# Expert weights of a mixture-of-experts stage: each 1 MB unit loaded by two 512 KB transfers with a semaphore each, waited for and freed by halves

## The reference, cut to what matters

```
def expert_choice_moe(h, w_router, w_gate, w_up, w_down):      # h: 1 x 512 x 1024
    cap = CAPACITY_FACTOR * S // N_EXPERTS                      # 64 rows for each of 16 experts
    aff = jax.nn.softmax((h @ w_router).astype(jnp.float32), axis=-1)
    gates, idx = lax.top_k(aff.swapaxes(1, 2), cap)
    xin = jax.vmap(lambda hb, ib: hb[ib])(h, idx)
    a = jnp.einsum("becd,edf->becf", xin, w_gate)               # each of the three weights is 1024 x 1024
    b = jnp.einsum("becd,edf->becf", xin, w_up)
    y = jnp.einsum("becf,efd->becd", jax.nn.silu(a) * b, w_down)
    y = y * gates.astype(y.dtype)[..., None]
    ... # rows are added back at idx; the last step of the program is an RMS norm of the result
```

## Time and profile before

| what | value |
|---|---|
| time, median of 3 runs | 2463.63 us (2462.45 to 2464.12) |
| the profiled execution's own time | 2466.73 us |
| its span, first to last instruction | 2464.9 us |
| TensorE busy | 2389.1 us, 97% of the span |
| DVE, ACT, POOL busy | 1211.2, 860.4 and 37.2 us |
| DMA | 387.64 MB, mean 157 GB/s over the span |
| transfers of units | 192 of 1024 KB |

### The profile page before, as it was taken

How to read it: one execution, slowest core, us unless ns; L and a number is a source line. 1 busy time by engine, 2 the same in 40 slices (tenths; PEclk the granted TensorE clock), 3 DMA queues, 4 the chain that set the end, 5 groups by cost and what they waited for, 6 DMA issues and landing times. The chain is left out here.

```text
span 2464.9 us, 34565 instructions
## 1 busy us (share of the span) xinstructions
PE 2389.1 (97%) x14242; PEld 1847.2 (75%) x14242; DVE 1211.2 (49%) x1867; ACT 860.4 (35%) x1325; POOL 37.2 (2%) x57
## 2 busy tenths in 40 slices
PE   6999999999999999999999999999998999999997
PEld 5994889999999988677788888876897753333323
DVE  3798556552455343674664565653543422233223
ACT  4125653321233233584542344356444311101101
POOL 0000000000000001100000000000000100000000
PEclk8999999999999999999999999999999999999999
DMA  5248432221112142002232232220341669999996
GB/s 232 86 125 306 172 119 86 68 83 47 60 61 80 65 164 83 31 2 69 94 101 96 94 104 93 82 62 1 107 145 41 256 279 408 421 421 421 421 421 286
DMA packets 74251, 387.64 MB, mean 157 GB/s; under 512 B 8576, under 2 KB 12928, under 8 KB 43264
## 3 DMA queue, kind: packets, MB, share of 16 engines
q1 hardware_dynamic: 74112, 385.66, 41.6%
HBM read 380.22 MB, written 2.10 MB: 155 GB/s over the span
## 5 line engine op out<-in xcount | busy, mean ns | idle before, releaser
L285 DVE TENSOR_TENSOR WLO<-RAW,WHI 128x1024 fp32r<-128x1024 f32 (+3 forms) x221 | 273.1, 1236 | 627.8 <-ACT WHI L272 627.7
L329 PE MATMUL PS<-XNH,WHI 128*128 128x384 f32 (+2 forms) x1816 | 572.7, 358 | 7.2 <-PEq L2839 2.6
L329 PE MATMUL PS<-XNH,WLO 128*128 128x384 f32 (+2 forms) x1816 | 564.8, 353 | 0.0
L329 PE MATMUL PS<-XNL,WHI 128*128 128x384 f32 (+2 forms) x1816 | 564.5, 353 | 0.0
L272 ACT ACTIVATE WHI<-RAW 128x1024 fp32r<-128x1024 f32 (+3 forms) x221 | 236.2, 1069 | 754.1 <-PE PS L329 715.1
L329 PEld LDWEIGHTS PS<-XNH,WHI 128*128 128x128 f32 x1816 | 335.3, 188 | 40.7 <-issue 10.0
L329 PEld LDWEIGHTS PS<-XNL,WHI 128*128 128x128 f32 x1816 | 335.2, 188 | 31.4 <-issue 3.4
L329 PEld LDWEIGHTS PS<-XNH,WLO 128*128 128x128 f32 x1816 | 335.1, 188 | 29.2
L3049 PE MATMUL PS<-RAWM,XS 128*64 128x512 f32 x1024 | 237.2, 599 | 9.0 <-DMA RAWM<-experts 8.4
L3049 PEld LDWEIGHTS PS<-RAWM,XS 128*64 128x64 f32 x1024 | 68.2, 136 | 139.2 <-issue 105.1
L329 PE MATMUL PS<-HH,WHI 128*128 128x384 f32 (+1 forms) x528 | 158.0, 353 | 0.1
(11 more groups left out here) (379 smaller groups left out, 2754.5 us busy)
## 6 DMA issues: line engine op xcount, KB each, us to landing
RAWM<-experts SPq DMA_DIRECT2D x191, 1024.0 KB, 15.0
RAW<-up SPq DMA_DIRECT2D x88, 512.0 KB, 3.3
ADAW<-ada SPq DMA_DIRECT2D x26, 1024.0 KB, 6.5
RAW<-down SPq DMA_DIRECT2D x32, 704.0 KB, 4.0
ADAG<-ada SPq DMA_DIRECT2D x14, 1024.0 KB, 11.3
RAW<-pw SPq DMA_DIRECT2D x24, 512.0 KB, 3.8
ADAL<-ada SPq DMA_DIRECT2D x8, 1024.0 KB, 6.3
RAW<-qkv SPq DMA_DIRECT2D x12, 512.0 KB, 3.5
```

The costliest lines, as they stand in the source:

```text
L285: dve.tensor_tensor(lo[:, 0:to.length], prog.RAW[:, at % RAWS, 0:to.length], f32(hi[:, 0:to.length]), ALU.subtract).then_inc(prog.weights_ ...
L329: last = pe.matmul(prog.PS[:, to, at:at + b - a], w, x[:, k, a:b], start=(k == 0 and n == 0), stop=(k == g.k - 1 and n == 2))
```

## The change

Each unit is loaded by two transfers. The first takes columns 0 to 1023 of all 128 partitions, the second columns 1024 to 2047, so that a partition's row in a transfer is 4 KB in place of 8 KB. Each half of a slot has a semaphore of its own (28 in place of 14). TensorE waits for a half ahead of the block that is in it, and adds one to `done` after each block; SP waits for half of the former unit ahead of each half's transfer. ACT's waits on `done` count twice as many. The arithmetic and its order are the same.

```diff
+def load_half(prog, sp, g, c):
+
+    moe = prog.moe
+    slot, src = moe.slots[g], prog.dram["experts"][g][:, c * UNIT // 2:(c + 1) * UNIT // 2]
+    to = moe.whole[slot]
+    if len(to.shape) == 3:
+        to, src = to[:, 4 * c:4 * c + 4, :], src.rearrange("p (a b) -> p a b", b=TOK - LAT)
+    else:
+        to = to[:, c * UNIT // 2:(c + 1) * UNIT // 2]
+    sp.dma_start(to, src).then_inc(prog.expert_landed[2 * slot + c], 16)
+
 def load_unit(prog, sp, g):
-    moe = prog.moe
-    slot, src = moe.slots[g], prog.dram["experts"][g]
-    if len(moe.whole[slot].shape) == 3:
-        src = src.rearrange("p (a b) -> p a b", b=TOK - LAT)
-    sp.dma_start(moe.whole[slot], src).then_inc(prog.expert_landed[slot], 16)
+    for c in range(2):
+        load_half(prog, sp, g, c)
...
             for g in range(N_SLOTS, UNITS):
-                sp.wait_ge(done, moe.before[g] + 1)
-                load_unit(prog, sp, g)
+                for c in range(2):
+                    sp.wait_ge(done, 2 * moe.before[g] + 1 + c)
+                    load_half(prog, sp, g, c)
...
             def unit(g, j, x, ps):
                 slot = moe.slots[g]
-                pe.wait_ge(prog.expert_landed[slot], 16 * moe.use[g])
                 for n in range(2):
+                    pe.wait_ge(prog.expert_landed[2 * slot + n], 16 * moe.use[g])
                     k = 2 * j + n
                     for half in range(2):
                         last = pe.matmul(ps[64 * half:64 * half + 64, :], x(k), moe.half[slot](2 * n + half),
                                          start=(k == 0), stop=(k == KD - 1))
-                last.then_inc(done, 1)
+                    last.then_inc(done, 1)
 
             def last_down(pair):
...
-                pe.wait_ge(prog.expert_landed[slot], 16 * moe.use[first_down(LAST_E) + pair])
                 for k in range(KD):
+                    if k % HALF_K == 0:
+                        pe.wait_ge(prog.expert_landed[2 * slot + k // HALF_K], 16 * moe.use[first_down(LAST_E) + pair])
...
-                last.then_inc(done, 1)
+                    if k % HALF_K == HALF_K - 1:
+                        last.then_inc(done, 1)
...
-                act.wait_ge(done, first_up(e) + PART)
+                act.wait_ge(done, 2 * (first_up(e) + PART))
```

More of the change, by code:

```diff
@@ L114, in __init__ @@
         self.gap_landed = nc_sem("ada_gap_landed")
-        self.expert_landed = [nc_sem(f"expert_landed{i}") for i in range(N_SLOTS)]
+        self.expert_landed = [nc_sem(f"expert_landed{i}") for i in range(2 * N_SLOTS)]
         first = self.expert_landed[-1].num + 1
@@ L3216, in _ @@
                 keep_rows(0, k)
-            act.wait_ge(done, PART)
+            act.wait_ge(done, 2 * (PART))
             act.activation(A[:], A_PS, ACT.Copy).then_inc(a_kept, 1)
@@ L3227, in _ @@
                 if e < LAST_E:
-                    act.wait_ge(done, first_gate(e + 1) + PART)
+                    act.wait_ge(done, 2 * (first_gate(e + 1) + PART))
                     act.activation(A[:], A_PS, ACT.Copy).then_inc(a_kept, 1)
-                    act.wait_ge(done, first_down(e) + PART)
+                    act.wait_ge(done, 2 * (first_down(e) + PART))
                     if e >= 1:
@@ L3245, in _ @@
                 cols = slice(pair * P, (pair + 1) * P)
-                act.wait_ge(done, first_down(LAST_E) + pair + 1)
+                act.wait_ge(done, 2 * (first_down(LAST_E) + pair + 1))
                 act.activation(YH_LAST[:, cols], LAST_Y_PS[pair][:, cols], ACT.Copy, scale=last_gate).then_inc(y_hi, 1)
```

## The result

| kernel | median | lowest and highest | runs |
|---|---|---|---|
| before | 2463.63 us | 2461.43 to 2464.78 | 5 |
| changed | 2472.74 us | 2470.91 to 2475.26 | 5 |

The changed kernel takes 1.0039 of the time before, with an interval of 1.0028 to 1.0049: 9.1 us more, where 6.4 were forecast.

The account below looks back on a forecast made before the run. The DMA engines, full at 421 GB/s in the experts' stage, were taken as the bound. The terms +8.4 - 0.9 - 1.1 = +6.4 us on the median of 2463.63 gave 2470.0 us, range 2463 to 2478.

Parts of the forecast that it names:

- The rate: Experts' stage: 4 KB packets make each of 178 units 47 ns slower on the DMA engines, +8.4 us.
- I take the mean of the three: Experts' unit cost: 23, 39 and 79 ns from three stretches of 4 KB packets, averaged to 47 ns.
- Rows cut out of longer rows: Experts' halves in HBM: 4 KB out of every 8 KB costs nothing; other end 6 ns a unit, +1.1 us.
- The first slot is free sooner: Start of the experts' stage: the queue starts to fill half a unit sooner and keeps that, -0.9 us.
- the end: Last up unit: half its work moves ahead of the last landing, and the rank rows' delay goes, -1.1 us.
- What is hidden: Experts' stage: 178 more SP issues at 328 ns, 0.66 us a unit, and TensorE's new waits should cost nothing.
- If that limit counts transfers: Full queue of some ten transfers: ten halves would still be 12.5 us of work, unseen by the engines.
- Smaller packets cost little: Rival, experts' transfers: 0 to 37 ns a unit, not slower; 2465.7 us at 23 ns, 2461.6 at nothing; chance 0.31.
- TensorE becomes the bound: Rival, experts' stage: each new wait costs TensorE 0.22 us, +38 us, 2501 us; chance 0.04.
- Each transfer's fixed time: Rival, experts' transfers: two 3.3 us transfers pass one after the other, 6.6 us a unit, +731 us; chance 0.02.
- The release sets the pace: Rival, last 115 us: the loop from release to landing binds, so halves gain 5.6 us, 2458 us; chance 0.03.
- What was to show it: Signs in the new profile's experts' stage: DMA share 1.0 or more, near 413 GB/s, an expert 30.5 us.

Follow-up runs that it names:

- halves_adjacent: The changed kernel, with each half of a unit as one block of 512 KB in HBM: 2472.66 us, 1.0033 of the kernel before.
- ends_only: The kernel before, with halves for unit 14 and units 184 to 187 only, whole units for all others: 2462.81 us, ratio 1.0001.
- halves_whole_waits: The changed kernel, with SP waiting for the whole former unit and TensorE for both halves (except the last four down units): 2476.44 us, 1.0062 of before.
- rows4k_one: The kernel before, one transfer a unit, with each partition's row as two 4 KB pieces far apart in HBM: 2472.40 us, ratio 1.0032.
- pairs: The kernel before, with neighbouring units from unit 58 on loaded by one 2 MB transfer, 16 KB rows: 2460.35 us, 0.9988; again 2461.90, 0.9994.

## Why the prediction was right, and what in it was off

**The rate.** The mechanism is the one given: the DMA engines set the pace, and smaller packets lower it for all units. The size was off. The term had 47 ns a unit; the chip took 74 in steady stretches and 72 over the 174 units up to unit 187. (The sum counted 178; the four down units behind that landing aren't on the path, 0.2 us.) The step that mis-sized it is "I take the mean of the three". Of the three stretches the third, the one that "lies behind a long full queue", had 2.630 us of packet time a unit, or 79 ns more after the overlap. The same working on the changed kernel (102.4% of 280 us times 16 engines, over 27,917 packets, times 16) gives 2.629 us. So the reason to take that stretch alone stood in the text, and two stretches of short bursts diluted it. With 79 ns the sum would have been 178 times 0.079 less 2.0, +12.1; with the measured 72 and 174 it is 12.5 less 1.8, +10.7, and the medians gave +9.1. The range of 2463 to 2478 held the result by its width, with a term that was a third too small.

**Rows cut out of longer rows.** Nothing was taken, and nothing it is: `halves_adjacent` has the same rate.

**The first slot is free sooner, and the end.** Forecast −0.9 and −1.1, found −0.86 at the first issue and −0.93 behind the landing of unit 187. Two steps behind these terms don't hold. The queue does not keep the early start to the end: in `ends_only` it was gone by unit 53, and in the kernel before, the queue isn't full from the start on, though the sum took it so (unit 51 landed 5.8 us after its issue). And the rank rows did hold up unit 187 before (it landed at 2432.33, forecast 2432.37, and was loaded at 2432.64), but they hold it up still, 0.66 us behind its first half. What the end gained came from unit 185, of which only half is left to do behind its last landing: 0.78 by the chains. That the sum of the term came out near is partly luck.

How far the two reach the end is less sure. From the first unit to the last up unit, two transfers with whole waits take 457.3 us (`halves_whole_waits`), and with halves 455.1 and 454.5 (changed, `halves_adjacent`): 2.2 and 2.8 us less. One transfer with the same 4 KB packets and whole waits takes 455.4 (`rows4k_one`), only 0.3 and 0.9 more than the halves. Of the 1.9 us between the two kernels with whole waits, 1.2 stand at unit 18, which landed 16.5 us behind the first issue with one transfer and 17.7 with two. So two transfers may have a price of their own at the stage's start, paid once and about as large as what the halves gain. It rests on one trace each, with executions that differ by more than a microsecond for other reasons, and isn't shown.

**What is hidden.** TensorE's waits in the middle of a unit are free where the data is there: 7.09 and 10.52 us as before. SP's issues became longer than forecast, since the queue holds some twelve halves and SP stands at it, but a DMA share of 1.03 says that nothing is lost. Its forecast of 0.66 us a unit for 178 more issues was the free price; the full queue makes it 2.14 for a unit's two. The limit doesn't count transfers, which the prediction had as a condition ("If that limit counts transfers"). With whole units of 4 KB rows SP stands at it too (`rows4k_one`, ns min/median/max of an issue, then landing):

```profile
L2989 SPq DMA_DIRECT2D RAWM<-experts x191: 367/567/5507, 1919.4 to 2433.5; - x191
...
DMA to landing us min/median/max: 4.9/18.2/21.7
```

At 2.566 us a unit, 21.7 us are some eight units, where it was ten with rows of 8 KB.

**The rivals.** *Smaller packets cost little* fell: 74 ns, where it ended at 37. The rule weighed there (the Trainium skill, DMA: Bandwidth & Descriptors, "Why small descriptors are slow (HBM only)") gave an estimate of 28 ns a unit from its 3 cycles a packet; the runs have 9.3 to 9.4 ns a packet in the place of its 3.5. The measurement decides. *TensorE becomes the bound* fell with the uncut pieces. *Each transfer's fixed time* fell with `rows4k_one`: one transfer or two, the same rate; a price paid once, at the start, stays open. *The release sets the pace* fell for the steady stretch, where earlier releases only made a queue longer that was full; early in the stage of the kernel before, where the queue is short, it isn't ruled out.

**What was to show it.** Share of 1.0 or more: 1.03. Rate near 413: 409. Chain over to transfers before 2315: 2248. An expert 30.5 us: 12 times 2.567, 30.8. First transfer 0.9 sooner: 0.86. Scatter 1 us less behind the landing: 0.93.

## What to carry to other kernels

Where a DMA share of 1.0 says that the queue is the bound, count packets before anything else: halving the row that a partition gets in a transfer added a fixed price a packet for every unit, and early starts by half a unit could pay once at most, at the ends, where the one at the front didn't last. When a price is to be read from stretches of a trace, take the one whose state is that of the stage to be changed (here a long full queue), not a mean with others. And a larger transfer hands over its first part only with its last: of the 3.3 us that pairs gained in the queue, 1.5 reached TensorE's last up unit.

## What the runs showed of the hardware that was not expected

- In a full queue a packet costs about 9.3 ns beyond its bytes, and the same from 16 KB rows to 2 KB rows: 426, 421, 409 and 387 GB/s for the mix with 16 KB, and for rows of 8, 4 and 2 KB. In that queue the number of transfers, and the pitch of the rows in HBM, changed the unit time by 1 ns or less.
- Two transfers of 64 partitions in place of one of 128, with the same rows of 8 KB, brought the rate from 421 to 247 GB/s at a DMA share of 1.02. Packets lasted 540 ns in place of 315.
- SP's issue isn't free at a full queue: 1072 ns in the median with halves of 4 KB rows in it, and up to 5507 with whole units of 4 KB rows, where it was 328 in the median, and at most 1667, with whole units of 8 KB rows. The queue held fewer bytes with the smaller rows: some eight units in place of ten.
